# x and a at other byte distances from the weights in the 272-column stages

## What is computed

```python
def swiglu(h, w_gu, w_down):
    g, u = jnp.split(h @ w_gu, 2, axis=-1)
    return (jax.nn.silu(g) * u) @ w_down

h = jnp.concatenate([meta, x], axis=1)              # 272 rows
for i in range(2):
    h = h + 0.5 * rms_norm(swiglu(rms_norm(h, g0), w_gu, w_down), g1)
    h = h + rms_norm(mixer_i(rms_norm(h, g2)), g3)  # convolution, then attention
    h = h + 0.5 * rms_norm(swiglu(rms_norm(h, g4), w_gu2, w_down2), g5)
x = h[:, 16:]                                       # 256 rows for the second block
```

## Time and profile before

| | |
|---|---|
| median of 3 runs | 1532.84 us (1532.22 to 1532.97) |
| the profiled execution | 1531.38 us |
| its span, from the first to the last instruction | 1529.5 us |
| TensorE (PE) busy | 1474.2 us, 96% |
| weight loads (PEld) busy | 1443.6 us, 94% |
| VectorE (DVE) busy | 1065.0 us, 70% |
| ScalarE (ACT) busy | 680.7 us, 45% |
| mean granted TensorE clock | 0.994 |

### The profile page before, as it was taken

How to read it: one execution, slowest core, us unless ns; L and a number is a source line. 1 busy time by engine, 2 the same in 40 slices (tenths; PEclk the granted TensorE clock), 3 DMA queues, 4 the chain that set the end, 5 groups by cost and what they waited for, 6 DMA issues and landing times. The chain is left out here.

```text
span 1529.5 us, 29328 instructions
## 1 busy us (share of the span) xinstructions
PE 1474.2 (96%) x12027; PEld 1443.6 (94%) x12027; DVE 1065.0 (70%) x1443; ACT 680.7 (45%) x809; POOL 28.9 (2%) x58
## 2 busy tenths in 40 slices
PE   5999999999999999999999979999999999999999
PEld 4999999999999999999988879999898989999999
DVE  5666878776667876677867676668877665776653
ACT  5443344354443454433545555443432535454441
POOL 0000100000000000000000000001000000000000
PEclk9999999999999999999999989999999999999999
DMA  7545745436447555457332135558343234454550
GB/s 295 188 166 191 262 179 193 165 105 244 174 165 251 217 193 184 173 196 286 141 131 107 60 138 193 201 187 302 149 142 134 84 117 179 173 188 170 176 209 29
DMA packets 41677, 269.14 MB, mean 176 GB/s; under 512 B 4672, under 2 KB 5824, under 8 KB 12272
## 3 DMA queue, kind: packets, MB, share of 16 engines
q1 hardware_dynamic: 33120, 240.31, 43.6%
q0 software_dynamic: 7312, 26.44, 4.9%
q10 hardware_dynamic: 1152, 1.05, 0.2%
HBM read 266.73 MB, written 1.05 MB: 175 GB/s over the span
## 5 line engine op out<-in xcount | busy, mean ns | idle before, releaser
L363 PE MATMUL ps<-x_hi,w_hi 128*128 128x272 f32 (+2 forms) x2488 | 725.1, 291 | 29.6 <-DVE w_lo L983 16.5
L364 PE MATMUL ps<-x_lo,w_hi 128*128 128x272 f32 (+2 forms) x2488 | 708.6, 285 | 0.0
L365 PE MATMUL ps<-x_hi,w_lo 128*128 128x272 f32 (+2 forms) x2488 | 708.5, 285 | 0.0
L1741 ACT ACTIVATE w_hi<-raw_weights 128x2048 fp32r<-128x2048 f32 x222 | 423.5, 1912 | 362.7 <-PE ps L365 362.5
L983 DVE TENSOR_TENSOR w_lo<-raw_weights,w_hi 128x2048 fp32r<-128x2048 f32 x196 | 447.1, 2290 | 167.3 <-ACT w_hi L1741 166.7
L363 PEld LDWEIGHTS ps<-x_hi,w_hi 128*128 128x128 f32 x2488 | 472.6, 190 | 37.8 <-DVE w_lo L983 16.5
L364 PEld LDWEIGHTS ps<-x_lo,w_hi 128*128 128x128 f32 x2488 | 473.0, 190 | 2.8 <-issue 2.4
L365 PEld LDWEIGHTS ps<-x_hi,w_lo 128*128 128x128 f32 x2488 | 472.5, 190 | 0.0
L363 PE MATMUL ps<-a_hi,w_hi 128*128 128x272 f32 x592 | 169.6, 286 | 0.0
L364 PE MATMUL ps<-a_lo,w_hi 128*128 128x272 f32 x592 | 169.6, 286 | 0.0
L365 PE MATMUL ps<-a_hi,w_lo 128*128 128x272 f32 x592 | 169.6, 286 | 0.0
(11 more groups left out here) (247 smaller groups left out, 1375.2 us busy)
## 6 DMA issues: line engine op xcount, KB each, us to landing
raw_weights<-w_units SPq DMA_DIRECT2D x228, 1024.0 KB, 4.9
mod_w<-mod_units POOLq DMA_DIRECT2D x48, 512.0 KB, 5.3
h<-x_in SPq DMA_DIRECT2D x1, 1088.0 KB, 5.5
out<-h ACTq DMA_DIRECT2D x8, 128.0 KB, 1.9
tab<-tables POOLq DMA_DIRECT2D x1, 512.0 KB, 10.0
tab<-constants POOLq DMA_DIRECT2D x1, 272.0 KB, 3.1
con<-constants POOLq DMA_DIRECT2D x2, 128.0 KB, 6.6
f<-constants POOLq DMA_DIRECT2D x1, 136.0 KB, 7.0
```

Source lines behind the costliest of these rows:

```text
L363: pe.matmul(dst, wh, hi, start=start, stop=False)
L364: pe.matmul(dst, wh, lo, start=False, stop=False)
L365: return pe.matmul(dst, wl, hi, start=False, stop=stop)
L1741: act.activation(w_hi[:, u % RING, :], raw[:, u % RING, :], ACT.Copy).then_inc(S["hi_ready"], 1)
```

## The change

In the 272-column stages x now lies 160 bytes (mod 256) past the weights, and a 96. `A_SHIFT = 160` moves `a_hi` and `a_lo` up by 160 bytes in the arena, which is 256 bytes longer so that the weights behind it keep their place mod 256; `mod_acc` moves with a's end. For x, the 192 bytes of `mod` ahead of it are replaced by an unused tensor of 160 bytes, and `mod` is put behind x.

The 256- and 258-column stages keep 192: `a_hi_s` and `a_lo_s` stay at the arena's start, and new tiles `x_hi_s`, `x_lo_s` lie 32 bytes after `x_hi`, `x_lo` in the same area. `x_of[T]` chooses between the two, in TensorE's calls, in VectorE's `update_and_prepare` and in ScalarE's `prepare`. What lies behind x (f, pair_a, pair_b, sq and the small tensors) moves by 160 bytes mod 256. No instruction, wait or transfer is added or removed, and no shape is changed.

```diff
--- before.py
+++ after.py
@@ -49,6 +49,7 @@
 PITCH = 320
+A_SHIFT, X_SHIFT = 160, 32
 V_LN = 0
@@ -166,17 +167,17 @@
         a_bytes = FT * PITCH * 4
-        acc_at = 2 * a_bytes - (PITCH - TOK) * 4
+        acc_at = A_SHIFT + 2 * a_bytes - (PITCH - TOK) * 4
         acc_bytes = MOD_PER * 256 * 4
 
-        sb("arena", [P, (acc_at + acc_bytes) // 4])
+        sb("arena", [P, (acc_at + acc_bytes + 256 - A_SHIFT) // 4])
 
 
-        a_hi = at("a_hi", 0, [P, FT, PITCH], F32R)
-        a_lo = at("a_lo", a_bytes, [P, FT, PITCH], F32R)
+        a_hi = at("a_hi", A_SHIFT, [P, FT, PITCH], F32R)
+        a_lo = at("a_lo", A_SHIFT + a_bytes, [P, FT, PITCH], F32R)
         a_hi_s = at("a_hi_s", 0, [P, FT, SEQ], F32R)
@@ -211,13 +212,17 @@
         h = sb("h", [P, KT, TOK])
-        mod = sb("mod", [P, 48])
+        sb("x_shift", [P, (192 - X_SHIFT) // 4])
         x_at = -(-nc.sbuf_base // 32) * 32
         x_lo = nc.alloc_sbuf_tensor_at("x_lo", [P, KT, PITCH], F32R, offset=x_at + x_bytes)
-
+        x_hi_s = nc.alloc_sbuf_tensor_at("x_hi_s", [P, KT, PITCH], F32R, offset=x_at + X_SHIFT)
+        x_lo_s = nc.alloc_sbuf_tensor_at("x_lo_s", [P, KT, PITCH], F32R, offset=x_at + x_bytes + X_SHIFT)
+        x_of = {TOK: (x_hi, x_lo), SEQ: (x_hi_s, x_lo_s)}
+
+        mod = sb("mod", [P, 48])
         f_at = -(-nc.sbuf_base // 32) * 32
@@ -540,7 +545,7 @@
                     bank_busy = lambda m: pe.wait_ge(S["h_ready"], H_UP4 + m + 1)
-                group(st, 0, (x_hi, x_lo), x_base=x_base, bank_busy=bank_busy, between=between)
+                group(st, 0, x_of[st.T], x_base=x_base, bank_busy=bank_busy, between=between)
 
@@ -548,15 +553,15 @@
                 c.up("rstd_kept")
-                group(st, 1, (x_hi, x_lo), bank_busy=lambda m: wait_side(part, m))
+                group(st, 1, x_of[st.T], bank_busy=lambda m: wait_side(part, m))
 
                 with pe.Fori(0, 4) as i:
-                    group(st, 2, (x_hi, x_lo), i)
-                    group(st, 3, (x_hi, x_lo), i)
-                group(st, 10, (x_hi, x_lo))
+                    group(st, 2, x_of[st.T], i)
+                    group(st, 3, x_of[st.T], i)
+                group(st, 10, x_of[st.T])
 
@@ -802,8 +807,8 @@
                             wait_bank(w_in, w_in.t0 + m)
-                        ins = three_pass(ps[:, m, 0:SEQ], u % RING, (k * 2 + m) * P, x_hi[:, k, 0:SEQ],
-                                         x_lo[:, k, 0:SEQ], k == 0, k == KT - 1)
+                        ins = three_pass(ps[:, m, 0:SEQ], u % RING, (k * 2 + m) * P, x_hi_s[:, k, 0:SEQ],
+                                         x_lo_s[:, k, 0:SEQ], k == 0, k == KT - 1)
                         if k == KT - 1:
@@ -924,7 +929,7 @@
             small_group()
-            xs = (x_hi, x_lo)
+            xs = x_of[SEQ]
             group(w_in, 0, xs, between={1: [lambda: key_and_weights()]})
@@ -1122,8 +1127,8 @@
                 dve.wait_ge(S["shift_ready"], 1)
-                dve.tensor_tensor(x_lo[:, :, SEQ:SEQ + 2], shift.unsqueeze(2).broadcast_to([P, KT, 2]),
-                                  x_hi[:, :, SEQ:SEQ + 2].bitcast(F32), ALU.subtract)
+                dve.tensor_tensor(x_lo_s[:, :, SEQ:SEQ + 2], shift.unsqueeze(2).broadcast_to([P, KT, 2]),
+                                  x_hi_s[:, :, SEQ:SEQ + 2].bitcast(F32), ALU.subtract)
 
@@ -1159,7 +1164,7 @@
                 last = 7 if deferred else 6
-                hi, lo = x_hi, x_lo
+                hi, lo = x_of[T]
                 for m in range(8 + 2):
@@ -1819,9 +1824,10 @@
                         act.activation(f[:, m, 0:T], ps[:, st.bank(st.t0 + m), 0:T], ACT.Copy).then_inc(S["f_kept"], 1)
-                prepare(T, off, next_gain, full, st.bank(st.t0), hi=x_hi)
-
-            def prepare(T, off, next_gain, full, bank, hi=x_hi, update=True, split_after=None):
+                prepare(T, off, next_gain, full, st.bank(st.t0))
+
+            def prepare(T, off, next_gain, full, bank, update=True, split_after=None):
+                hi = x_of[T][0]
                 for m in range(8):
@@ -2137,7 +2143,7 @@
             act.wait_ge(S["mod_evicted"], MOD_PARTS)
-            act.activation(x_hi[:, :, SEQ:SEQ + 2], mod[:, 24:32].unsqueeze(2).broadcast_to([P, KT, 2]), ACT.Copy)\
+            act.activation(x_hi_s[:, :, SEQ:SEQ + 2], mod[:, 24:32].unsqueeze(2).broadcast_to([P, KT, 2]), ACT.Copy)\
                .then_inc(S["shift_ready"], 1)
```

## The result

The changed kernel takes 1538.34 us, the kernel before in the same comparison 1532.97 us (medians of 15 runs each). The ratio, formed from the runs and not from the two medians (which are 5.4 us apart), is 1.0023, with a 95% interval of 1.0012 to 1.0034: slower by 3.5 us (1.8 to 5.2), where 20.7 us less was forecast. The sign and the size are both wrong. One run of the changed kernel, of 2094.8 us at a mean granted clock of 0.65, is not in the ratio.

A forecast was written before the change was run, and what follows sets the result against it. TensorE's matmul spacing was taken as the bound. Savings of 14.7 us (x) and 6.0 us (a), all other terms 0, gave 1532.84 - 20.7 = 1512.1 us, range 1489 to 1547.

The forecast's parts named there:

- What bounds the kernel: Whole kernel: no engine or transfer holds TensorE up in the body; time is its 6096 272-column matmuls times their spacing.
- the 7.6 ns over the bfloat16 filler: Every 272-column fp32r matmul: 123.4 ns against the filler's 115.8, read as two SBUF reads meeting; at most 46 us to win.
- parts a and b: 272-column stages: x to 160 saves 14.7 us over 4320 matmuls, a to 96 saves 6.0 us over 1776.
- the level under the present one: 272-column matmuls in x and a: spacing falls from 123.4 to 120.0 ns, the 258-column row's, -3.4 ns each.
- bound of +5.9 from above: 272-column matmuls: the most the spacing could grow, in ns each, taken from 258 columns' extra cost over 256.
- Nearly all goes: Rival, 272-column stages: the reads no longer meet, 117 ns, -6.4 each, 39 us less, 1493.8 us; chance 0.26.
- The distance is not the cause: Rival: fp32r streams beside 512-byte loads cost the excess wherever they lie; time stays at 1532.8 us; chance 0.12.
- Slower: one more piece to read: Rival, x and a: starting 32 bytes off a 64-byte multiple touches 18 pieces, +2.4 ns each, 14.6 us, 1547.4 us; chance 0.20.
- Cover (c): Stages with faster TensorE: VectorE, ScalarE and weight transfers still keep up, cost 0; 5.4 us lost if not in down stages.
- Part d: 256- and 258-column stages: 0, but a changed rhythm may move part of w_in between 117.7 and 113.3, 1.6 us either way.
- Part e: f, pair_a, pair_b, sq and small tensors, moved by 160 bytes mod 256: cost 0, 1 us either way.
- 0.68 for faster: Whole kernel: chance of a faster result, from one level down (0.42) and nearly all of the excess gone (0.26).

The follow-up runs named there:

- the layout alone: The changed kernel with both shifts set to zero and the rest of the new layout kept, against the kernel before: ratio 0.9996 (0.9980 to 1.0012).

## Why the prediction was wrong, point by point

**What bounds the kernel** was right: TensorE's spacing sets the time, and every ns in it came through to the end (with x at 128 and a at 224 the trace is longer by 19.5 us, where the spacings give 20).

**The step that failed** is the one that read the 7.6 ns over the bfloat16 filler as the loss of two reads that meet. It rested on "load 111.6 and stream 115.8 are both below 123.4; together they are slower than either". But the 115.8 were of a bfloat16 stream, taken for an fp32r stream, and no row had an fp32r stream beside a short load. With 32 weight columns it is as slow (124.8 at 192), and its excess grows with its length (17.6 ns at 512 columns), so the 7.6 ns are the pace of the fp32r stream and not a loss to the load, as far as loads of a quarter can show it. What the meeting of load and stream does cost comes on top, 0 to 3.9 ns by distance, and at 192 it was already the least of all tested. So the gain that could be had was not 46 us: none at any tested distance, and about 6096 x 0.3 = 1.8 us by the estimate of 123.1. The way that was open was to a longer spacing.

**The price of the change** (parts a and b) took 120.0 ns from the 258 columns as "the level under the present one". That row was the pace of another length. At its best distances 258 columns take 119.9 and 272 take 123.3; the levels aren't a ladder that one stream climbs. For x the measured term is 0.1 ns or less in the gate-up stages, not -3.4; for a it is +2.0, not -3.4. The bound of +5.9 from above held: the dearest distance of 272 columns cost +3.9 (127.2, at 216).

**The rivals.** "Nearly all goes" falls with the same step. "The distance is not the cause" is false as a mechanism (123.3 to 127.2 by distance alone), yet its result was the right one for x. By the rule of the Trainium skill (SBUF - State Buffer, "Who interferes with whom"), that TensorE never waits on anyone and its two read ports are independent, all the distances would be alike; the runs contradict the independence for 4-byte operands, by up to 3.9 ns in 123.3, and agree for bfloat16 (115.8 at five distances). The formula N / 2.4 + 2.5 of the Trainium skill (TensorE: Matmul & The Clock Gate, "Back-to-back issue gap"), which that section gives for an isolated matmul, held for bfloat16 (115.8 at 272 columns, and 215.8 by the formula against 215.9 at 512) and not for fp32r (215.8 against 233.4). "Slower: one more piece to read" had the right sign, and with +2.4 ns a price near a's +2.0, for a wrong reason: x at 160 begins as far off a multiple of 64 as a at 96 and costs nothing, and a pair with both operands moved by 32 bytes keeps its spacing. It priced both tiles, 14.6 us; one was hit. The measured 1538.3 us lies inside the stated range only because the range went up to this rival's price; the forecast's own reasoning has no part in that.

**Cover (c)** was right: no new wait. It wasn't tested at a faster TensorE. Down 0 wasn't the stage with the most VectorE work for its length, as it says: conv_in with its tail has 66.3 of 81.3 us. **Part d** foresaw that 256-column stretches may change between 113.3 and 117.7, but in w_in alone, and allowed 1.6 us for it; w_in came out 2.9 us longer, and in another trace gate-up 3 and down 3 show 6.7. **Part e** put the new places of f and the rest at 0, 1 us either way; nothing speaks against it, but the interval for the layout alone, 0.9980 to 1.0012, is wider (3 us less to 2 us more).

**Slips in the working** that change nothing: (1.92 - 0.25) / 15 is 111.3 and not 111.6, and the four spacings 113.3, 117.7, 120.0 and 123.4 lie 2.3 to 4.4 ns apart, not 3.3 to 6.7.

**The chances.** 0.68 for faster hung on one reading that no row at a second distance supported. The rows gave spacings of 256, 258 and 272 columns, all at 192, and nothing on the sign of a move. The kernel before already stood at the best of the tested distances, and no row could show that.

## What to carry to other kernels

Before an excess over a formula is taken for a stall that can be removed, look for a row of the same data type that is free of the suspected partner; a filler in another type is no floor. Where the distance of two tiles mod 256 matters, TensorE alone with all distances in one kernel gives the ranking in one run. It carried over to the full kernel, to 0.1 ns for 192, 160 and 128; 96 came out 1.2 ns dearer in some stages, as a distance with a second level can. Change one tile's distance at a time: here the x half was harmless and the a half lost everything.

## What the runs showed of the hardware

An fp32r stream of 512 columns takes 231.7 to 233.4 ns, with 32 and with 128 weight columns, about 0.4525 ns a column, where bfloat16 at the same granted clock of 2.4 GHz takes 215.9. It isn't quite even: 256 columns can take 113.3, less than their share of 115.8, and 248 take 116.7.

At one distance and length the stream can settle at different spacings when it starts, and then keeps the one it has. In the kernel that varied the columns, 96 matmuls of 256 columns came after 1 to 8 tiny ones: 118.6 ns after 1, 2, 3, 5 and 7, and 114.3 after 4, 6 and 8, with nothing between. Each of these has a first step of some 200 ns in it. Without it they are at 117.8 and 113.3, the two levels of the full kernels: (10.53 - 0.28) / 87 and (9.91 - 0.28) / 85 in the second block below, which has the same stretches in narrower windows. Each number of tiny matmuls was tried once, so it isn't shown that the number decides.

```profile
331.96 11.55 PE L207 MATMUL ps<-mov,wts 128*128 128x256 f32 x96
343.35 0.50 PE L209 MATMUL ps<-mov,wts 128*128 128x2 f32 x4
343.72 11.14 PE L212 MATMUL ps<-mov,wts 128*128 128x256 f32 x96
```

```profile
332.75 10.53 PE L207 MATMUL ps<-mov,wts 128*128 128x256 f32 x88
...
344.26 9.91 PE L212 MATMUL ps<-mov,wts 128*128 128x256 f32 x86
```

In a full kernel this can hold for whole stages. With a alone shifted, the profiled execution ran down 3 at 62.20 us for 528 matmuls, 117.8 ns, where before it took 59.90:

```profile
1032.90:1095.10 62.20, 62.20 (x530) 1.00 0.76 279
```

Gate-up 3 was at the same level. In that execution 20 of its matmuls start 2.24 us apart in 19 steps, 117.9 ns; the kernel before has 708 matmuls in 80.00 us there (two or three reach in from before), 113.3 ns.

```profile
949.73 0.28 PE L370 MATMUL ps<-x_hi_s,w_lo 128*128 128x256 f32 x1
...
951.97 0.28 PE L368 MATMUL ps<-x_hi_s,w_hi 128*128 128x256 f32 x1
```

```profile
930.00:1010.00 80.00, 80.00 (x708) 1.00 0.54 190
```

Gate-up 3 is 4.4 us longer by this (134.01 against 129.66 us in the table of stages), and with down 3's 2.3 us it is 6.7. Of 63 runs of the kernel before, 34 took 1532 to 1535 us and 19 took 1536 to 1542, about that much apart, which would fit; but no trace was taken of one of the longer runs, so this stays open. Open too is what in the chip sets the pace of a 4-byte stream, and why 160, 176 and 192 are good distances and 184 isn't.
